# Down weights in output halves, a written-out layer loop and a router on column groups in a two-layer encoder

## The chip, the cores and the metric

The kernel runs on one core of one Trainium2 chip. The metric is the device time of one execution in microseconds. The kernel before took 2113.52 us, the median of three runs (2112.22 to 2116.02).

## The reference

The model has two layers on 256 tokens of 1024 numbers, all in float32. Each layer adds an attention branch and a long-convolution branch to x, and then an expert network. The part that the change touches is the second:

```python
def expert_choice_ffn(h, router_w, wg, wu, wd):       # h = rms_norm(x), 256 x 1024
    C = 32                                            # tokens per expert, 16 experts
    aff = softmax(h @ router_w)                       # 256 x 16
    gate, idx = top_k(aff of each expert over the tokens, C)
    xs = h[idx]                                       # 16 x 32 x 1024
    a = einsum('becd,edf->becf', xs, wg)              # f = 1408
    u = einsum('becd,edf->becf', xs, wu)
    o = einsum('becf,efd->becd', silu(a) * u, wd) * gate
    return zeros(256, 1024).at[idx].add(o)            # added to the tokens
```

Each expert chooses its 32 tokens; the three weight matrices of an expert (gate, up and down) hold 1024 x 1408 numbers each.

## The kernel before

The kernel is written engine by engine: each engine has a program of its own, with waits on semaphores between them. In each of these programs the layer loop is a hardware loop (`Fori(0, DEPTH)`), so a wait in it compares with a value worked out in registers, such as `L * 16 + 4 * it + 1`.

A layer has a dense part (latents, projections, attention, convolution by DFT, branches, output product) and an expert part. x stays in SBUF as two blocks of 128 tokens. The dense weights pass through a ring; the same memory holds an expert's gate and up weights later (`ring`), and `region` holds its down weights.

**Router** (lines 629 to 670). The normalized tokens are transposed block by block: DVE (L1200) and ACT (L892) write `aT`, eight blocks of 128 features by 256 tokens. L654 forms the logits as a product of 16 output rows, eight blocks accumulated in one bank, two records of TensorE for each block. DVE copies the 16 x 256 result (L1206), two transposes bring it back to tokens by experts (L660), softmax and top-k follow on DVE and ACT, and L670 and L1241 give the table from which L681 gathers the tokens of a group of four experts.

**Experts.** A loop over four groups holds four experts each, in TensorE's and DVE's programs; ACT and SP loop over the experts. For an expert TensorE forms gate and up products (L695) in 4 column groups of 32 (the 1408 columns are 3+3+3+2 blocks of 128), ACT takes silu (L920), DVE multiplies (L1262), three transposes (L709) and a DVE copy (L1266) give `hT`. The down product (L719) walks b = 0, 1, 2 over the 11 row blocks, 4 + 4 + 3, and for each b over both output halves c, 44 records in all (two for each of 22 products). For each b it waits for one piece of the down weights:

```python
for b in range(FB):
    pe.wait_ge(wd_in[b], 16 * n + 16)
    for c in range(2):
        for j in range(len(TILES[b])):
```

Then ACT copies output half 0 (L926) and DVE half 1 (L1268), and L734 combines: four products (eight records) with `gselT`, the gate values placed by token, in the order token block 0 halves 0 and 1, token block 1 halves 0 and 1. DVE adds each to x (L1273). The next layer's ACT program waits until the first two of the last four adds are done, issues three small loads for the filters (L762, L764), and squares the two token blocks (L769); the root (L772) releases DVE's reciprocal (L980).

**Loads.** SP issues the expert weights in this order: first half of gate of expert e when half of the gate product of e-1 is done, second half when all of it is, up (L272) when the up product is done, and the three down pieces (L278) when the down product is done (`o_psum`). The first down load of a layer goes out in the dense part, gate and up of expert 0 when the ring is free.

Of the kernel before, what the change touches and what calls it, by code (L numbers as in the profile page):

```python
# [14 lines left out]
ALU = mybir.AluOpType  # L15
# [4 lines left out]
P = 128  # L20
D, S, DEPTH = 1024, 256, 2
SB, DB = S // P, D // P
# [11 lines left out]
FB = 3  # L34
# [6 lines left out]
HW = 512  # L41
EPS = 1e-6
# [33 lines left out]
C_N = C_EPS + 1  # L76
# [14 lines left out]
W_N = DB + DB * E  # L91


def build(nc, x_in, vecs, fvecs, qkw_in, consts_in, decay_in, w_lat, w_q_b, units_in,
          filt12, filt3, w_gate, w_up, w_down, out):
    with ExitStack() as ctx:
# [70 lines left out]
        lgT = uT_t[0:E, 4096:4096 + S]  # L167
# [42 lines left out]
        wd = R[:, 0:NF_TILES * D].rearrange("p (r d) -> p r d", r=NF_TILES)  # L210
# [13 lines left out]
        o_psum o_act o_dve y2_psum x_dve""".split()  # L224
# [8 lines left out]
        def _(sp):  # L233
            sp.dma_start(x3, x_in.rearrange("a (b p) d -> p (a b) d", p=P)).then_inc(s["x_in"], 16)
            sp.dma_start(cst[:, :], consts_in).then_inc(s["consts_in"], 16)
            with sp.Fori(0, DEPTH) as L:
# [37 lines left out]
                def load_down(e):  # L274

                    for b in range(FB):
                        cols = slice(CT * D * b, CT * D * b + len(TILES[b]) * D)
                        sp.dma_start(R[:, cols], w_down[L * E + e, :, cols]).then_inc(wd_in[b], 16)  # L278
# [32 lines left out]
        def _(pool):  # L311
            with pool.Fori(0, DEPTH) as L:
# [32 lines left out]
        def _(pe):  # L345
# [5 lines left out]
            with pe.Fori(0, DEPTH) as L:  # L351
# [298 lines left out]
                for i in range(DB):  # L650
                    if i % 4 == 0:
                        pe.wait_ge(s["xn2T_dve"], 2 * L + 1 + i // 4)
                        pe.wait_ge(s["xn2T_act"], 2 * L + 1 + i // 4)
                    m = mm(bank(4, S, rows=E), fvec[:, W_RT + i * E:W_RT + (i + 1) * E], aT[:, i],  # L654
                           start=i == 0, stop=i == DB - 1)
# [3 lines left out]
                for t in range(SB):  # L659
                    m = tp(bank(5, E, t * E), lgT[:, t * P:(t + 1) * P], ident[0:E, 0:E])  # L660
# [13 lines left out]
                with pe.Fori(0, NG) as g:  # L674
# [11 lines left out]
                    for q in range(GROUP):  # L686
# [24 lines left out]

                        pe.wait_ge(s["hT_dve"], n + 1)
                        pe.wait_ge(s["o_act"], n + FREE)
                        pe.wait_ge(s["o_dve"], n + FREE)
                        for b in range(FB):
                            pe.wait_ge(wd_in[b], 16 * n + 16)
                            for c in range(2):
                                for j in range(len(TILES[b])):
                                    m = mm(bank(c, rows=CAP, row0=CAP * j),  # L719
                                           hT[:, b * P + CAP * j:b * P + CAP * (j + 1)],  # L720
                                           wd[:, CT * b + j, c * 512:(c + 1) * 512], start=b == 0,
                                           stop=j >= len(TILES[b + 1]) if b < FB - 1 else True)
                        m.then_inc(s["o_psum"], 1)

                        pe.wait_ge(s["gselT_act"], n + 1)
                        for k in range(4):
                            t, c = k // 2, k % 2
                            if k == 0:
                                pe.wait_ge(s["o_act"], n + 1 + FREE)
                            if k == 1:  # L730
                                pe.wait_ge(s["o_dve"], n + 1 + FREE)

                            pe.wait_ge(s["x_dve"], n * 4 + max(k - 1, 0) + X_FREE)
                            mm(bank(6 + k % 2), gselT[:, t * P:(t + 1) * P], o_sb[:, c * 512:(c + 1) * 512],  # L734
                               start=True, stop=True).then_inc(s["y2_psum"], 1)
# [3 lines left out]
        def _(act):  # L739
# [17 lines left out]
            with act.Fori(0, DEPTH) as L:  # L757
# [3 lines left out]
                act.wait_ge(s["x_dve"], L * E * 4 + X_FREE - 2)  # L761
# [154 lines left out]
                with act.Fori(0, E) as e:  # L916
                    n = L * E + e
                    act.wait_ge(s["gate_done"], n + 1 + FREE)
                    act.wait_ge(s["hid_dve"], n + FREE)
                    af(sil[:, 0:2 * P], bank(2, 2 * P), ACT.Silu)  # L920
                    af(sil[0:ROWS_LAST, 2 * P:FT], bank(2, P, 2 * P, rows=ROWS_LAST),
                       ACT.Silu).then_inc(s["sil_act"], 1)
                    act.wait_ge(s["gselT_psum"], n + 1)
                    af(gselT, bank(4, S), ACT.Copy).then_inc(s["gselT_act"], 1)  # L924
                    act.wait_ge(s["o_psum"], n + 1 + FREE)
                    af(o_sb[:, 0:512], bank(0), ACT.Copy).then_inc(s["o_act"], 1)  # L926
# [3 lines left out]
        def _(dve):  # L930
# [46 lines left out]
            with dve.Fori(0, DEPTH) as L:  # L977
# [228 lines left out]
                copy(lgT, bank(4, S, rows=E)).then_inc(s["lgT_dve"], 1)  # L1206
# [31 lines left out]
                with dve.Fori(0, NG) as g:  # L1238
# [13 lines left out]
                    for q in range(GROUP):  # L1252
# [14 lines left out]
                        dve.wait_ge(s["o_psum"], n + 1 + FREE)  # L1267
                        copy(o_sb[:, 512:1024], bank(1)).then_inc(s["o_dve"], 1)  # L1268
                        for k in range(4):
                            t, c = k // 2, k % 2  # L1270
                            dve.wait_ge(s["y2_psum"], n * 4 + k + 1)
                            xc = x3[:, t, c * 512:(c + 1) * 512]
                            tt(xc, xc, bank(6 + k % 2), ALU.add).then_inc(s["x_dve"], 1)  # L1273


def constants():
# [26 lines left out]
    c[:, C_EPS] = EPS  # L1303
    tau = np.abs(pos - S // 2) / f32(S // 2)
# [72 lines left out]
```

## Time and profile before

| | before |
|---|---|
| median of three runs | 2113.52 us |
| profiled execution | 2112.32 us |
| its span, first to last instruction | 2110.5 us |
| TensorE busy | 1606.2 us (76%) |
| DVE busy | 508.7 us (24%) |
| ACT busy | 287.6 us (14%) |
| moved by DMA | 644.83 MB, mean 306 GB/s |
| instructions recorded | 23405 |

The first layer runs to about 1055 us: its dense part ends at about 411 us, the router and the gather at about 433 us, and the experts fill the rest. The second layer repeats this. PE is TensorE's matmul record and PEld its weight load, which lies beside it; PEclk is the clock that TensorE was granted, 1.00 being full speed and 0.50 half. "Idle before" names what ended an engine's wait; where it says "issue", the engine waited for nothing that the profile shows.

### The profile page before, as it was taken

To read this page: it belongs to the slowest core of one execution; us is meant where nothing else is said; L and a number is where in the kernel's file an instruction comes from. 1 tells how busy PE (TensorE), PEld (TensorE's weight loads), DVE (VectorE), ACT (ScalarE), POOL (GpSimd) and SP (SyncE) were. 2 spreads that over 40 slices of the span, in tenths; PEclk is the share of its full clock that TensorE was granted. 3 is DMA by queue.
4 is the path that set the end of the run, shared out by engine and by line. 5 is a ranking of instruction groups with operands and counts; after the bars stand their busy time and mean duration, and the time that the engine had idled before them with its cause. 6 is when DMAs were issued, how large, how long until landed. Compare 5 with 4: busy or idle time off the path is not lost.

```text
span 2110.5 us, 23405 instructions
## 1 busy us (share of the span) xinstructions
PE 1606.2 (76%) x9552; PEld 909.9 (43%) x9552; DVE 508.7 (24%) x1057; ACT 287.6 (14%) x594; POOL 45.7 (2%) x24
## 2 busy tenths in 40 slices
PE   7999999876466566666689999997865665665665
PEld 4687688432232132232256866884322222321322
DVE  2654541111111111111126545402111111111111
ACT  2233200200000000000022332002000000000000
POOL 0300000000000000000002000000000000000000
PEclk9999999988788888878899999999887887888888
DMA  7522024679999999999945220246899999999997
GB/s 282 195 85 100 1 80 190 245 319 430 435 423 430 430 427 430 432 429 426 426 149 199 80 100 1 80 189 258 341 434 426 426 430 434 423 430 430 427 430 319
DMA packets 36352, 644.83 MB, mean 306 GB/s; under 512 B 3984, under 2 KB 4880, under 8 KB 6160
## 3 DMA queue, kind: packets, MB, share of 16 engines
q1 hardware_dynamic: 35472, 638.84, 72.2%
q10 hardware_dynamic: 768, 4.29, 0.7%
q8 instruction: 96, 1.57, 0.3%
q14 instruction: 16, 0.13, 0.0%
HBM read 642.07 MB, written 1.05 MB: 305 GB/s over the span
## 4 chain that ended last, share of the span: by engine, by line
PE 49%; DMA 42%; issue 4%; DVE 3%; DVEq 1%; SPq 1%; ACT 1%; ACTq 0%
DMA region<-w_down_dram 27%; DMA ring<-w_up_dram 15%; PE ps L695 7%; PE ps L394 7%; PE ps L619 5%; PE ps L461 5%; PE ps L719 3%; PE ps L644 3%; PE ps L552 2%; PE ps L681 2%; PE ps L587 2%; PE ps L577 2%; PE ps L422 2%; PE ps L484 1%; PE ps L439 1%
## 5 line engine op out<-in xcount | busy, mean ns | idle before, releaser
L695 PE MATMUL ps<-ring,uT 128*32 128x384 f32 (+1 forms) x4096 | 437.7, 567 | 296.8 <-DMA ring<-w_gate_dram 147.6
L695 PEld LDWEIGHTS ps<-ring,uT 128*32 128x32 f32 x4096 | 182.9, 130 | 550.6 <-issue 205.6
L719 PE MATMUL ps<-region,uT 128*32 128x512 f32 x1408 | 175.8, 596 | 34.9 <-DVE uT L1266 22.2
L1262 DVE TENSOR_TENSOR uT<-uT,ps 128x256 f32<-128x256 f32 x32 | 13.5, 421 | 699.4 <-PE ps L695 699.4
L394 PE MATMUL ps<-xnT,ring 128*128 128x256 f32 x768 | 178.3, 380 | 4.5 <-DVE uT L942 2.9
L394 PEld LDWEIGHTS ps<-xnT,ring 128*128 128x128 f32 x768 | 140.6, 190 | 24.1 <-DVE uT L942 4.5
L734 PE MATMUL ps<-uT 128*128 128x512 f32 x256 | 124.3, 618 | 28.8 <-ACT uT L926 28.8
L920 ACT ACT_TABLE_LOAD x32 | 41.1, 1283 | 631.3 <-PE ps L695 631.3
L461 PE MATMUL ps<-xnT,ring 128*128 128x256 f32 x512 | 115.0, 380 | 0.0
L719 PEld LDWEIGHTS ps<-region,uT 128*32 128x32 f32 x1408 | 44.5, 109 | 143.9 <-issue 105.3
L1273 DVE TENSOR_TENSOR x<-x,ps 128x512 f32<-128x512 f32 x128 | 87.9, 687 | 64.4 <-PE ps L734 64.4
L681 PE MATMUL ps<-uT,xnT 128*128 128x128 f32 x256 | 50.5, 381 | 68.2 <-issue 65.6
L461 PEld LDWEIGHTS ps<-xnT,ring 128*128 128x128 f32 x512 | 96.5, 190 | 13.7 <-issue 0.8
L734 PEld LDWEIGHTS ps<-uT 128*128 128x128 f32 x256 | 40.7, 188 | 114.9 <-issue 73.0
L681 PEld LDWEIGHTS ps<-uT,xnT 128*128 128x128 f32 x256 | 48.7, 294 | 73.7 <-issue 73.7
L1268 DVE COPY uT<-ps 128x512 f32<-128x512 f32 x32 | 22.1, 691 | 194.5 <-PE ps L719 194.5
L619 PE MATMUL ps<-uT,ring 128*128 128x256 f32 x256 | 57.9, 379 | 0.0
L619 PE MATMUL ps<-attnT,ring 128*128 128x256 f32 x256 | 57.9, 379 | 0.0
L644 PE MATMUL ps<-ring,uT 128*128 128x512 f32 x128 | 55.6, 592 | 0.0
L924 ACT ACTIVATE uT<-ps 128x256 f32<-128x256 f32 x32 | 12.3, 384 | 311.6 <-PE ps L703 311.6
L619 PEld LDWEIGHTS ps<-uT,ring 128*128 128x128 f32 x256 | 48.6, 190 | 6.6
L619 PEld LDWEIGHTS ps<-attnT,ring 128*128 128x128 f32 x256 | 48.6, 190 | 6.6
(195 smaller groups left out, 1368.1 us busy)
## 6 DMA issues: line engine op xcount, KB each, us to landing
ring<-w_gate_dram SPq DMA_DIRECT2D x64, 2816.0 KB, 28.4
ring<-w_up_dram SPq DMA_DIRECT2D x32, 5632.0 KB, 32.8
region<-w_down_dram SPq DMA_DIRECT2D x64, 2048.0 KB, 30.6
ring<-units_dram SPq DMA_DIRECT2D x34, 2048.0 KB, 8.0
region<-w_down_dram SPq DMA_DIRECT2D x32, 1536.0 KB, 37.2
ring<-w_lat_dram SPq DMA_DIRECT2D x4, 1344.0 KB, 20.6
ring<-w_q_b_dram SPq DMA_DIRECT2D x2, 2304.0 KB, 29.1
region<-filt_dram ACTq DMA_DIRECT2D x4, 512.0 KB, 11.9
```

Of the source, the lines that this page charges most:

```text
L394: m = mm(bank(b % 2, S), unit8(n)[:, i, j * P:(j + 1) * P], xnT[:, i], start=i == 0, stop=i == DB - 1)
L422: m = mm(bank((3 + g) % 7), latT[:, i, t * P:(t + 1) * P], m2[:, i, c * 512:(c + 1) * 512], start=i == 0, stop=i == QB - 1)
L461: m = mm(dst, unit8(7 + 4 * (i // 4) + g)[:, k, i % 4 * P:(i % 4 + 1) * P], xnT[:, k], start=k == 0, stop=k == DB - 1)
L552: m = mm(bank(5 + f), cst[:, C_F + t * NF + f * P:C_F + t * NF + (f + 1) * P], hflt[:, t], start=t == 0, stop=t == SB - 1)
L577: m = mm(bank(2 + f), cst[:, C_F + t * NF + f * P:C_F + t * NF + (f + 1) * P], z_t[:, c, t], start=t == 0, stop=t == SB - 1)
L619: m = mm(dst, unit8(n)[:, k, j * P:(j + 1) * P], (aT if g == 2 else uT)[:, k], start=k == 0, stop=k == DB - 1)
L644: m = mm(bank(4 + 2 * c + t), mT[:, k, t * P:(t + 1) * P], unit8(n)[:, k], start=k == 0, stop=k == DB - 1)
L681: m = mm(bank(i // 4, P, (i % 4) * P), xn2[:, t, i * P:(i + 1) * P], pick[:, t], start=t == 0, stop=t == SB - 1)
L695: m = mm(bank(b, QW[j], rows=CAP, row0=CAP * j), xs[:, i, q * CAP:(q + 1) * CAP], w[:, i, j * FT:j * FT + QW[j]], start=i == 0, stop=i == ...
L719: m = mm(bank(c, rows=CAP, row0=CAP * j), hT[:, b * P + CAP * j:b * P + CAP * (j + 1)], wd[:, CT * b + j, c * 512:(c + 1) * 512], start=b ...
L734: mm(bank(6 + k % 2), gselT[:, t * P:(t + 1) * P], o_sb[:, c * 512:(c + 1) * 512], start=True, stop=True).then_inc(s["y2_psum"], 1)
L1273: tt(xc, xc, bank(6 + k % 2), ALU.add).then_inc(s["x_dve"], 1)
```

## The change

It has three parts, and some that follow from them.

1. The down weights lie in memory by output halves (half, row block, column), and come in three pieces: all 11 row blocks of half 0; the first 8 of half 1; the last 3 of half 1. TensorE forms all of half 0, ACT copies it, TensorE combines it with both token blocks, and then comes half 1 in the same way with DVE's copy. The combination's order is now half 0 for token blocks 0 and 1, then half 1. ACT's first wait of a layer is for three of the last four adds.
2. `for L in range(DEPTH)` takes the place of the hardware loop in all five programs: the code of both layers stands one behind the other, and L is a constant. The loops over experts and groups stay.
3. The router's weights are padded from 16 to 32 columns. Feature block i goes to column group i % 4, so four partial sums stand in four groups of 32 rows; a product with a 128 x 16 matrix of zeros and ones adds them up and turns them at once, in place of the two transposes.

With this, the router weights and the constants get wider, and the reserved scratch memory for DMA descriptors goes down to 2048.

```diff
+WD_AT = [0, NF_TILES * HW, (NF_TILES + 2 * CT) * HW, 2 * NF_TILES * HW]
+C_SUM = C_EPS + 1
+C_N = C_SUM + E
+EP = 32
+W_N = DB + DB * EP
-        wd = R[:, 0:NF_TILES * D].rearrange("p (r d) -> p r d", r=NF_TILES)
+        wd = R[:, 0:NF_TILES * D].rearrange("p (c r d) -> p c r d", c=2, r=NF_TILES)
...
-            with sp.Fori(0, DEPTH) as L:
+            for L in range(DEPTH):
...
-                    for b in range(FB):
-                        cols = slice(CT * D * b, CT * D * b + len(TILES[b]) * D)
-                        sp.dma_start(R[:, cols], w_down[L * E + e, :, cols]).then_inc(wd_in[b], 16)
+                    for k in range(3):
+                        cols = slice(WD_AT[k], WD_AT[k + 1])
+                        sp.dma_start(R[:, cols], w_down[L * E + e, :, cols]).then_inc(wd_in[k], 16)
...
-                    m = mm(bank(4, S, rows=E), fvec[:, W_RT + i * E:W_RT + (i + 1) * E], aT[:, i],
-                           start=i == 0, stop=i == DB - 1)
+                    m = mm(bank(4, S, rows=EP, row0=EP * (i % 4)), fvec[:, W_RT + i * EP:W_RT + (i + 1) * EP], aT[:, i],
+                           start=i < 4, stop=i >= 4)
...
-                    m = tp(bank(5, E, t * E), lgT[:, t * P:(t + 1) * P], ident[0:E, 0:E])
+                    m = mm(bank(5, E, t * E), lgT[:, t * P:(t + 1) * P], cst[:, C_SUM:C_SUM + E], start=True, stop=True)
...
+                        def down(c, b):
+                            for j in range(len(TILES[b])):
+                                m = mm(bank(c, rows=CAP, row0=CAP * j),
+                                       hT[:, b * P + CAP * j:b * P + CAP * (j + 1)],
+                                       wd[:, c, CT * b + j], start=b == 0,
+                                       stop=j >= len(TILES[b + 1]) if b < FB - 1 else True)
+                            return m
+                        def combine(c):
+                            for t in range(SB):
+                                k = 2 * c + t
+                                pe.wait_ge(s["x_dve"], n * 4 + max(k - 1, 0) + X_FREE)
+                                mm(bank(6 + t), gselT[:, t * P:(t + 1) * P], o_sb[:, c * 512:(c + 1) * 512],
+                                   start=True, stop=True).then_inc(s["y2_psum"], 1)
                         pe.wait_ge(s["hT_dve"], n + 1)
                         pe.wait_ge(s["o_act"], n + FREE)
+                        pe.wait_ge(wd_in[0], 16 * n + 16)
+                        for b in range(FB):
+                            m = down(0, b)
+                        m.then_inc(s["oa_psum"], 1)
+                        pe.wait_ge(s["gselT_act"], n + 1)
+                        pe.wait_ge(s["o_act"], n + 1 + FREE)
+                        combine(0)
                         pe.wait_ge(s["o_dve"], n + FREE)
+                        pe.wait_ge(wd_in[1], 16 * n + 16)
                         for b in range(FB):
-                            pe.wait_ge(wd_in[b], 16 * n + 16)
...
+                            if b == FB - 1:
+                                pe.wait_ge(wd_in[2], 16 * n + 16)
+                            m = down(1, b)
                         m.then_inc(s["o_psum"], 1)
...
+                        pe.wait_ge(s["o_dve"], n + 1 + FREE)
+                        combine(1)
...
-                act.wait_ge(s["x_dve"], L * E * 4 + X_FREE - 2)
+                act.wait_ge(s["x_dve"], L * E * 4 + X_FREE - 1)
...
-                    act.wait_ge(s["o_psum"], n + 1 + FREE)
+                    act.wait_ge(s["oa_psum"], n + 1)
...
-                copy(lgT, bank(4, S, rows=E)).then_inc(s["lgT_dve"], 1)
+                copy(lgT, bank(4, S)).then_inc(s["lgT_dve"], 1)
...
-    nc = bacc.Bacc("TRN2", target_bir_lowering=False, num_devices=1)
+    nc = bacc.Bacc("TRN2", target_bir_lowering=False, num_devices=1, dynamic_dma_scratch_size=2048)
```

## Rows read from the trace of the kernel before

**Rows 1.** The page's DMA load, mean busy share in 40 equal slices of the span.
```profile
DMA  7522024679999999999945220246899999999997
```
**Rows 2.** By stage: window, length, busy us (records) of five engines, PEclk, DMA, GB/s.
```profile
91.00:192.00 101.00, 100.22 (x545) 83.19 (x545) 53.43 (x127) 39.51 (x107) 0.00 (x0) 1.00 0.24 86
...
432.90:1047.80 614.90, 396.60 (x3038) 158.99 (x3038) 83.16 (x166) 44.34 (x79) 0.00 (x0) 0.84 1.00 426
1047.80:1062.46 14.66, 5.79 (x20) 1.66 (x21) 5.02 (x8) 4.57 (x8) 0.00 (x0) 0.87 1.02 376
```
**Rows 3.** The chain of waits, two loads of down weights: start, us, what.
```profile
604.81 37.34 DMA region<-w_down_dram
...
645.19 37.53 DMA region<-w_down_dram
```
**Rows 4.** Windows of 4 us ahead of the first expert, columns as in rows 2.
```profile
424.00:428.00 4.00, 2.50 (x12) 2.45 (x13) 0.73 (x4) 0.00 (x0) 0.00 (x0) 0.50 0.02 4
428.00:432.00 4.00, 3.89 (x24) 3.70 (x23) 0.76 (x2) 0.00 (x0) 0.00 (x0) 0.68 0.00 0
```
**Rows 5.** Timeline, router to first expert: start, us, engine, line, what, [idle before].
```profile
410.78 3.61 PE L654 MATMUL ps<-attnT,fvec 128*16 128x256 f32 x16 [0.17 <-issue]
411.33 0.84 ACT L892 ACTIVATE attnT<-ps,fvec 128x256 f32<-128x256 f32 x2
...
414.43 0.41 DVE L1206 COPY uT<-ps 16x256 f32<-16x256 f32 x1 [1.70 <-PE ps L654]
...
414.99 0.27 PE L660 MATMUL ps<-consts,uT 16*128 16x16 f32 x2 [0.60 <-DVE uT L1206]
...
425.87 6.03 PE L681 MATMUL ps<-uT,xnT 128*128 128x128 f32 x32 [1.31 <-DVE uT L1241]
...
432.86 10.52 PE L695 MATMUL ps<-ring,uT 128*32 128x384 f32 x128 [0.97 <-DVE uT L1248]
```
**Rows 6.** Groups by line and shape: busy us, mean ns of one, idle before.
```profile
L695 PE MATMUL ps<-ring,uT 128*32 128x256 f32 x1024 | 373.1, 487 | 0.0
...
L719 PE MATMUL ps<-region,uT 128*32 128x512 f32 x1408 | 175.8, 596 | 34.9 <-DVE uT L1266 22.2 <-DMA region<-w_down_dram 12.4
```
**Rows 7.** Timeline, last expert of layer one and start of layer two.
```profile
1043.53 3.64 PE L719 MATMUL ps<-region,uT 128*32 128x512 f32 x32 [0.69 <-DVE uT L1266]
...
1047.79 1.92 PE L719 MATMUL ps<-region,uT 128*32 128x512 f32 x12 [0.63 <-DMA region<-w_down_dram]
...
1049.77 0.60 ACT L926 ACTIVATE uT<-ps 128x512 f32<-128x512 f32 x1 [7.49 <-PE ps L719]
...
1050.60 3.88 PE L734 MATMUL ps<-uT 128*128 128x512 f32 x8 [0.90 <-ACT uT L926]
...
1051.76 0.69 DVE L1273 TENSOR_TENSOR x<-x,ps 128x512 f32<-128x512 f32 x1 [1.30 <-PE ps L734]
...
1052.62 0.69 DVE L1273 TENSOR_TENSOR x<-x,ps 128x512 f32<-128x512 f32 x1 [0.17 <-PE ps L734]
...
1053.48 0.51 ACTq L762 DMA_DIRECT2D region<-filt_dram  x1
...
1054.53 0.69 DVE L1273 TENSOR_TENSOR x<-x,ps 128x512 f32<-128x512 f32 x1 [0.17 <-PE ps L734]
1055.33 1.06 ACT L769 ACTIVATE work<-x 128x1024 f32<-128x1024 f32 x1 [3.45 <-DVE x L1273]
...
1057.59 0.30 ACT L772 ACTIVATE small<-small,consts 128x2 f32<-128x2 f32 x1
1060.73 0.17 DVE L980 RECIPROCAL small<-small 128x2 f32<-128x2 f32 x1 [5.52 <-issue]
```
**Rows 8.** Timeline, the last expert of layer two.
```profile
2094.65 3.64 PE L719 MATMUL ps<-region,uT 128*32 128x512 f32 x32 [0.69 <-DVE uT L1266]
...
2098.58 1.92 PE L719 MATMUL ps<-region,uT 128*32 128x512 f32 x12 [0.29 <-DMA region<-w_down_dram]
...
2105.41 0.69 DVE L1273 TENSOR_TENSOR x<-x,ps 128x512 f32<-128x512 f32 x1 [0.17 <-PE ps L734]
```

More of the change, by code:

```diff
@@ L166, in build @@
         hT = uT_t[:, 2816 + 2 * FT:2816 + 3 * FT]
-        lgT = uT_t[0:E, 4096:4096 + S]
+        lgT = uT_t[:, 4096:4096 + S]
         work = uT_t[0:E, 4352:4352 + S]
@@ L223, in build @@
         pick_dve xs_psum xs_dve gsel_dve gselT_psum gselT_act gate_half gate_done up_done sil_act hid_dve hT_psum hT_dve
[L224 removed]
+        oa_psum o_psum o_act o_dve y2_psum x_dve""".split()
         s = {n: sem(n) for n in names}
@@ L311, in _ @@
         def _(pool):
-            with pool.Fori(0, DEPTH) as L:
+            for L in range(DEPTH):
                 pool.wait_ge(s["qkw_scaled"], L + 1)
@@ L350, in _ @@
                 pe.sem_inc(s[n], FREE)
-            with pe.Fori(0, DEPTH) as L:
+            for L in range(DEPTH):
                 pe.wait_ge(s["consts_in"], 16)
@@ L717, in _ @@
[L717 to L722, printed above, removed]
-                        m.then_inc(s["o_psum"], 1)
@@ L725, in _ @@
[L725 to L735, printed above, removed]
+                            if b == FB - 1:
+                                pe.wait_ge(wd_in[2], 16 * n + 16)
@@ L756, in _ @@
                 act.sem_inc(s[n], FREE)
-            with act.Fori(0, DEPTH) as L:
+            for L in range(DEPTH):
                 load_sqrt_table()
-                act.wait_ge(s["x_dve"], L * E * 4 + X_FREE - 2)
+                act.wait_ge(s["x_dve"], L * E * 4 + X_FREE - 1)
                 act.dma_start(w12, filt12[L]).then_inc(s["filt_in"], 16)
@@ L976, in _ @@
             dve.sem_inc(s["x_dve"], X_FREE)
-            with dve.Fori(0, DEPTH) as L:
+            for L in range(DEPTH):
                 dve.wait_ge(s["norm1_rms"], L + 1)
@@ L1266, in _ @@
                         copy(hT[:, 0:2 * P + ROWS_LAST], bank(5, 2 * P + ROWS_LAST)).then_inc(s["hT_dve"], 1)
[L1267 to L1273, printed above, removed]
+                        for c in range(2):
+                            if c == 1:
+                                dve.wait_ge(s["o_psum"], n + 1 + FREE)
+                                copy(o_sb[:, 512:1024], bank(1)).then_inc(s["o_dve"], 1)
+                            for t in range(SB):
+                                dve.wait_ge(s["y2_psum"], n * 4 + 2 * c + t + 1)
+                                xc = x3[:, t, c * 512:(c + 1) * 512]
+                                tt(xc, xc, bank(6 + t), ALU.add).then_inc(s["x_dve"], 1)
 def constants():
@@ L1303, in constants @@
     c[:, C_EPS] = EPS
+    c[:, C_SUM:C_SUM + E] = np.arange(P)[:, None] % EP == np.arange(E)[None]
     tau = np.abs(pos - S // 2) / f32(S // 2)
@@ L1330, in k_major_experts, with by_halves @@
         return w.transpose(0, 2, 1, 3).reshape(DEPTH * E, P, -1)
+    def by_halves(w):
+        return w.reshape(DEPTH * E, P, NF_TILES, 2, HW).transpose(0, 1, 3, 2, 4).reshape(DEPTH * E, P, -1)
     small = np.zeros((DEPTH, P, 4), np.float32)
@@ L1337 @@
                            cols(a["filt_skip"].reshape(DEPTH, -1)), small], 2)
-    fvecs = np.concatenate([cols(a["norm2_w"]), k_major(a["router_w"]).reshape(DEPTH, P, -1)], 2)
+    router = np.pad(k_major(a["router_w"]), ((0, 0), (0, 0), (0, 0), (0, EP - E)))
+    fvecs = np.concatenate([cols(a["norm2_w"]), router.reshape(DEPTH, P, -1)], 2)
     qkw = np.concatenate([a["q_norm_w"], a["k_norm_w"]], 1)
@@ L1364 @@
         "w_gate": k_major_experts(a["expert_w_gate"], range(DB)), "w_up": k_major_experts(a["expert_w_up"], range(DB)),
-        "w_down": k_major_experts(a["expert_w_down"], [r for tiles in TILES for r in tiles]),
+        "w_down": by_halves(k_major_experts(a["expert_w_down"], [r for tiles in TILES for r in tiles])),
     }
-    nc = bacc.Bacc("TRN2", target_bir_lowering=False, num_devices=1)
+    nc = bacc.Bacc("TRN2", target_bir_lowering=False, num_devices=1, dynamic_dma_scratch_size=2048)
     arrays, args = {}, []
```

2 lines of the change are left out of this document (removed).

## The prediction

> **What bounds the kernel now.** I read the load row of the page first: the DMA queues are full from about 440 to 1050 us and again from about 1490 to the end [rows 1]. The table by stage then splits a layer in two. In the dense part TensorE is the bound: 100.2 of 101.0 us in the attention stretch. In the expert part the DMA is: 614.9 us at a DMA share of 1.00 and 426 GB/s, TensorE busy 396.6 of them [rows 2]. The chain of waits agrees: it runs from one load of down weights to the next, issued at 604.81 and at 645.19, 40.38 us apart [rows 3]. Each spends 37.3 us from issue to landing, nearly all behind the gate and up weights of its queue: an expert moves 3 x 5.77 MB = 17.3 MB, and 17.3 MB at 426 GB/s are 40.6 us. So inside the 15 refills of a layer only bytes count, and the change keeps the bytes and the number of pieces.
>
> Time can therefore move in three places: where TensorE, DVE and ACT hand the router's result on while the DMA idles (0.02 and 0.00 share in the two windows [rows 4]), behind the last landing of each layer, and at the border between the layers.
>
> **The router.** The stream of expert weights starts when half of the first gate product is done, so the router's microseconds count one for one. Before, 16 records take 3.61 us from 410.78, so they end at 414.39 [rows 5]. In four column groups the first eight have their inputs at once. The last eight wait for the scaled copies of ACT, two blocks from 411.33 to 412.17 [rows 5]. What eight records of 128x256 in column groups cost is not shown alone. Bounds: one record's 0.49 us if all overlap [rows 6], and 8 x 3.61/16 = 1.81 us if nothing does. Between them stands the first expert, 128 such records in 10.52 us, 0.082 each [rows 5]: seven more behind the first give 0.49 + 0.57 = 1.06, which I take. The end is then 412.2 + 1.06 = 413.3, 1.1 us sooner (bounds 1.7 and 0.4). The two small transposes become two products with full-height weights, four records for two: 0.27 us [rows 5] becomes 0.54, so +0.3 (between 0 and, at 0.23 a record, +0.6). DVE's copy grows in partitions, not in length: nothing. Net -0.85 us a layer, -1.7 in all, from -3.4 to about +0.4. If the four groups bring nothing, the second half also starts at 412.6, not 412.2.
>
> The Trainium skill (TensorEngine Tiling (Array Packing), Theoretical Speedup) gives up to 4x for a dimension of 32 or less. By it 3.61 us would become 0.9 and 2.7 us a layer would go; the ACT copy that ends at 412.17 is why I don't follow it: the engine could be four times faster and still not have its input.
>
> The granted clock blurs this. It is 0.50 in 424 to 428 and 0.68 in 428 to 432 [rows 4]: the upper level came back in mid-gather, about 4.6 us into the 6.03 us that start at 425.87. If it comes back at the same moment after a gather that starts earlier, the gather's head start is spent at half rate, and a layer keeps 0.4 of 0.85 us; if it comes back from the start, up to 2.3 us more go. On average I leave the 0.85.
>
> **Down weights by output halves.** Per expert the bytes are the same (5.77 MB), in pieces of 2.88, 2.10 and 0.79 MB for 2.10, 2.10 and 1.57. So at 426 GB/s the first half lands 6.8 us ahead of the end, the second piece 1.9 us ahead. In 15 of 16 experts all this lies beside a full DMA. In the last of each layer it is on the path, so I schedule TensorE there [rows 7].
> - Today: 32 records from 1043.53, which end at 1047.17; the last piece is in at 1047.79, 12 records take 1.92; ACT copies 0.60; the combination starts at 1050.60, and its four adds end at 1055.22.
> - After: the first half, 22 records. A record takes (3.64 - 0.59)/31 = 0.098 us, the last 0.59 [rows 6, 7]; so 2.66 us, 1043.53 to 1046.19. Handoff 0.06 and ACT copy 0.60: 1046.85. Handoff 0.23: the first combination starts at 1047.08. Four of the eight records: 1.94, to 1049.02. Only then come the second half's 22 records, queued behind the combination: 2.66, to 1051.68. Its weights landed at 1047.79, so they have waited for TensorE, not it for them. Handoff 0.06, DVE copy 0.69 (as an add of that shape), handoff 0.23: 1052.66. First add 1.16 later, 1053.82 to 1054.51; the second 0.86 after it, ending at 1055.37.
>
> That is 0.15 us later than today's 1055.22. The halves save the combination's first 1.94 us behind the landing, but they bring a wait for ACT's copy (0.89 us) into the middle of TensorE's order. hT is ready only 4.26 us before the last landing, and the first half with its combination needs 5.5. In the last layer it is ready 3.93 us before [rows 8]: 2094.65 + 11.84 = 2106.49 against 2106.10, +0.4 us. Queued behind the added wait is the second half, and behind that SP, which issues the next expert's down load about 1.9 us later than now; gate and up weights (11.5 MB, 27 us at 426 GB/s) cover this.
>
> **The border of the layers.** Today DVE ends its last add at 1055.22 and then waits for no semaphore that the profile shows: its reciprocal starts at 1060.73, "issue" [rows 7], though ACT's square root was done at about 1057.9: the first square at 1055.33, two of 1.06 with their accumulator reads (0.19 each, overlapped by 0.1), the root of 0.30. I read this as fetching the loop's first instructions after the jump back. Written out, DVE has no jump there. Then the roots decide. ACT's filter loads wait for the first token block: today that is the second add, ended 1053.31, issue at 1053.48, squares at 1055.33, 2.0 us behind the add. After, the first block is complete with the third add, 1054.51, so squares start at 1056.53, the root ends at 1059.1, DVE starts at about 1059.2: -1.5 us. If the stall stays, it starts with the later add and costs +0.15. TensorE's own jump lies under the wait for DVE and gives nothing.
>
> The Trainium skill (Runtime: NRT & Kernel Launch, Instruction fetch mechanics) says that a taken branch out of the two resident pages stalls on a fetch and that straight code is prefetched. By it the 5.5 us of DVE vanish whole, and TensorE's too; the sum keeps 1.5 of them, since ACT is late next.
>
> **Constants for register sums in waits.** The sums are formed while the engine still waits, and TensorE fills 99% of the attention stretch: nothing, at best 1 us in all. Wider router weights and constants add 64 KB and 8 KB of loads: under 0.1 us. The smaller scratch buffer serves no queue that the page lists.
>
> **Sum**, against the profiled execution (span 2110.5, 1.8 around it, 2112.32): -1.7 + 0.4 - 1.5 = -2.8 us (the first layer's end is inside the border's -1.5). That execution is 1.2 below the median of 2113.52, which I shift: 2110.7.
>
> **Rivals.**
> - The halves work as drawn: the first is combined before the second lands. Then only 3 x 2 records (about 1.0 against 1.92 us) and half the combination (1.94) follow the landing: 0.9 + 1.9 a layer, 5.6 in all, so near 2105. For it: the first half does land 6.8 us early. Against: hT starts at 1043.53, too late for 5.5 us of work. With a clock that returns early in the gather the same time is reached otherwise.
> - The stall moves rather than goes: DVE falls out of its expert loop into code not yet fetched. Then -1.7 + 0.4 + 0.15, near 2112.4.
> - Slower by late loads: SP issues down(e+1) only when the second half is done, 1.9 us later in each of 15 refills per layer. If the 37.3 us from issue to landing were latency, not queueing, the period of 40.38 us would grow by 1.9: 30 x 1.9 = +57 us, near 2170. It decides once the delay eats the queue behind it, 27 us of gate and up weights. Against: DMA share 1.00.
> - Slower by code: twice the pages, and a second copy of loops at another place in them. A loop that straddles what is resident stalls by DVE's 5.5 us per pass; in the expert part that is hidden for a few, in a dense part each such stall shows. One or two: +5 to +11, near 2118.
>
> **How the numbers follow.** My case has 0.50, the moved stall 0.14, the working halves or an early clock 0.24, late loads 0.04, code stalls 0.08. About 0.2%, 4.2 us, is what this measurement tells from no change, so faster means below 2109.3: the working halves or early clock, and the quarter of my case in which the clock favours one gather by 1.5 us or more: 0.36. Slower (above 2117.7): 0.04 and most of the code case, 0.09. Same: 0.55. The range for 8 in 10 goes from 2105.0 (halves work) to 2115.5 (router bounds at their bad end, moved stall, a bad clock in one gather).
>
> **What would show it.** Right: the same 40.3 to 40.4 us between down loads; the router's product ending about 1 us behind ACT's last scaled copy, set by that copy; in the last expert of a layer TensorE's second half starting after the first combination and after its weights landed; DVE without "issue" at the border. Wrong: a DMA share under 0.98 in the expert part, a gap between the first combination and the second half that waits for the DMA, new idle on "issue" in the second layer's dense part, or a dense part shorter by more than 1 us.

## The result and the profile after

The changed kernel takes 2101.66 us (median of 11 runs, 2098.29 to 2109.72), the kernel before 2112.26 (11 runs, 2109.29 to 2116.02). The ratio is 0.995, 95% interval 0.9937 to 0.9963: 10.6 us faster, between 7.8 and 13.3. The forecast was 2110.7 us, 2.8 us faster than the median then known, in a range from 2105.0 to 2115.5. The direction was right; the size was not. The time lies outside the range, and below 2109.3, where the prediction saw a chance of 0.36. The profiled execution took 2101.75 us, 10.6 less than the one of before.

Both profiled executions are divided at the same events: TensorE's first router product, its first gather product, its first gate product, the last packet of the layer's last up load, and the next layer's first transpose.

| stretch, us | before | after | change | forecast |
|---|---|---|---|---|
| start to router, layer one | 410.78 | 413.23 | +2.45 | 0 |
| router to gather | 15.09 | 14.16 | -0.93 | -0.85 |
| gather to first gate product | 6.99 | 7.60 | +0.61 | clock |
| first gate product to last up packet | 600.90 | 599.00 | -1.91 | 0 |
| to the first transpose of layer two | 28.69 | 26.68 | -2.01 | -1.5 |
| to router, layer two | 399.33 | 396.50 | -2.83 | 0 |
| router to gather | 15.07 | 13.93 | -1.14 | -0.85 |
| gather to first gate product | 7.15 | 6.34 | -0.81 | clock |
| first gate product to last up packet | 600.67 | 596.00 | -4.67 | 0 |
| to the end | 25.86 | 26.51 | +0.65 | +0.4 |

Together, what I had priced (router, border and end) came close to its price: -3.4 us for -2.8. What I had priced at nothing, the stretch in which the DMA is full, gave 6.6 us. The dense parts moved by +2.5 and -2.8 and cancel; over the 14 profiled kernels of this study they lie between 409.7 and 414.9 us and between 396.2 and 402.4, whatever the kernel.

The page's section on the DMA queues has what I had passed over. The instruction queue, packets, MB and share of 16 engines, before:

```profile
q8 instruction: 96, 1.57, 0.3%
```

and after:

```profile
q8 instruction: 48, 0.79, 0.2%
```

The packets are 16 KB each, and each takes 1.07 us (the median in the kernel before). Before, 30 of them lie in the 14 periods between the up weights of the layer's second expert and those of its last, in both layers; after, 12 in layer one and 4 in layer two. The length of these 14 periods can be read from the waits of TensorE's up product, which starts when the last part of the up load is in. The timeline of the kernel before (start, us, engine, line, what, idle before and what ended it), layer one and layer two:

```profile
466.18 3.42 PE L695 MATMUL ps<-ring,uT 128*32 128x384 f32 x22 [5.30 <-DMA ring<-w_up_dram]
...
1034.25 7.24 PE L695 MATMUL ps<-ring,uT 128*32 128x384 f32 x62 [6.24 <-DMA ring<-w_up_dram]
...
1517.47 2.14 PE L695 MATMUL ps<-ring,uT 128*32 128x384 f32 x13 [5.45 <-DMA ring<-w_up_dram]
...
2085.20 2.36 PE L695 MATMUL ps<-ring,uT 128*32 128x384 f32 x14 [6.08 <-DMA ring<-w_up_dram]
```

568.07 and 567.73 us. The same of the changed kernel, where the line is L698:

```profile
468.56 0.86 PE L698 MATMUL ps<-ring,uT 128*32 128x384 f32 x4 [4.53 <-DMA ring<-w_up_dram]
...
1034.47 6.82 PE L698 MATMUL ps<-ring,uT 128*32 128x384 f32 x64 [6.67 <-DMA ring<-w_up_dram]
...
1510.86 7.05 PE L698 MATMUL ps<-ring,uT 128*32 128x384 f32 x64 [4.36 <-DMA ring<-w_up_dram]
...
2073.94 7.61 PE L698 MATMUL ps<-ring,uT 128*32 128x384 f32 x64 [5.88 <-DMA ring<-w_up_dram]
```

565.91 and 563.08 us. The DMA is full in both ([rows 2] for before; the windows of after, columns as there):

```profile
434.99:1043.30 608.31, 390.16 (x3004) 152.17 (x3004) 83.10 (x167) 44.32 (x79) 0.00 (x0) 0.86 1.00 426
1477.44:2083.60 606.16, 392.85 (x3006) 151.91 (x3006) 83.11 (x167) 44.32 (x79) 0.00 (x0) 0.86 1.00 427
```

Where is the difference, if the DMA is full in both? In the spread over its 16 engines. The first packet of the up loads comes every 40.2 us in both kernels (before: 450.74 for expert 1, 1013.43 for expert 15, 562.7 us over 14). The last packet falls behind: before it comes 14.9 us after the first for expert 1 (465.68) and 20.3 us after it for expert 15 (1033.77). A load is complete only when its slowest part is in: expert 15's lands at 1034.20, and TensorE's product starts at 1034.25. A mean share of 1.00 does not show how far that part is behind.

The trace has 16 landing events for each up load, and they show the spread directly. Before, those of expert 1 in layer one lie within 1.7 us. Those of expert 15 lie in two groups: eight within 1.4 us, and eight that come 6.1 to 6.9 us after the first; layer two shows the same (1.4, and 6.2 to 6.8). In the changed kernel, layer one has eight within 0.4 us, one at 1.7, six at 3.2 to 3.5 and one at 5.0 us; in layer two all 16 lie within 1.9 us. So half of the parts fall behind, and further in the kernel with more packets.

TensorE's own fetch stalls went with the packets. The gather's group of the page, before:

```profile
L681 PE MATMUL ps<-uT,xnT 128*128 128x128 f32 x256 | 50.5, 381 | 68.2 <-issue 65.6
```

and after:

```profile
L684 PE MATMUL ps<-uT,xnT 128*128 128x128 f32 x256 | 37.0, 312 | 15.9 <-DVE uT L1253 9.3
```

The last expert of layer one and the border, in the timeline of after. These lines answer to [rows 7]:

```profile
1043.32 2.78 PE L717 MATMUL ps<-region,uT 128*32 128x512 f32 x22 [0.69 <-DVE uT L1278]
...
1046.99 1.98 PE L727 MATMUL ps<-uT 128*128 128x512 f32 x4 [0.89 <-ACT uT L938]
...
1048.90 2.77 PE L717 MATMUL ps<-region,uT 128*32 128x512 f32 x22
...
1051.73 0.69 DVE L1282 COPY uT<-ps 128x512 f32<-128x512 f32 x1 [2.04 <-PE ps L717]
...
1058.85 0.17 DVE L992 RECIPROCAL small<-small 128x2 f32<-128x2 f32 x1 [3.59 <-ACT small L784]
```

The second half's products start right behind the first combination, with no wait for weights, as scheduled. DVE's wait is now for ACT's root and no longer for "issue".

The router's product in layer one of the changed kernel, its second eight records and the four that add the partial sums up:

```profile
414.77 0.64 PE L657 MATMUL ps<-attnT,fvec 128*32 128x256 f32 x8 [0.89 <-ACT attnT L904]
...
416.03 0.81 PE L663 MATMUL ps<-consts,uT 128*128 128x16 f32 x4 [0.63 <-DVE uT L1218]
```

### The profile page after: what moved, and what is told of

It reads as the page before. It is cut to its first block, busy times and chain, and to the rows that moved or that the text cites. A ratio compares the mean times of both kernels' runs of the same rounds, so it can differ in the third digit from the quotient of the medians.

```text
span 2100.0 us, 22784 instructions
## 1 busy us (share of the span) xinstructions
PE 1600.1 (76%) x9556; PEld 896.8 (43%) x9556; DVE 508.3 (24%) x1057; ACT 287.4 (14%) x594; POOL 45.7 (2%) x24
## 4 chain that ended last, share of the span: by engine, by line
PE 48%; DMA 47%; DVE 2%; ACT 1%; DVEq 1%; issue 1%; SPq 0%; ACTq 0%
DMA ring<-w_up_dram 46%; PE ps L698 12%; PE ps L397 7%; PE ps L622 5%; PE ps L464 5%; PE ps L647 3%; PE ps L555 2%; PE ps L590 2%; PE ps L580 2%; PE ps L425 2%; PE ps L487 1%; PE ps L442 1%; PE ps L370 1%; DMA ring<-w_lat_dram 1%; PE ps L511 1%; PE ps L479 1%
## 5 line engine op out<-in xcount | busy, mean ns | idle before, releaser
L698 PE MATMUL ps<-ring,uT 128*32 128x384 f32 (+1 forms) x4096 | 446.5, 575 | 330.2 <-DMA ring<-w_up_dram 182.2
L698 PEld LDWEIGHTS ps<-ring,uT 128*32 128x32 f32 x4096 | 182.7, 132 | 593.0 <-issue 212.0
L464 PEld LDWEIGHTS ps<-xnT,ring 128*128 128x128 f32 x512 | 96.5, 190 | 13.7 <-issue 0.8
L684 PE MATMUL ps<-uT,xnT 128*128 128x128 f32 x256 | 37.0, 312 | 15.9 <-DVE uT L1253 9.3
L555 PE MATMUL ps<-work,consts 128*128 128x512 f32 x96 | 45.0, 620 | 4.1 <-DVE work L1120 4.1
L590 PE MATMUL ps<-consts,work 128*128 128x256 f32 x192 | 43.0, 380 | 2.3 <-DVE work L1166 2.3
```

What stands on the lines that cost most here:

```text
L464: m = mm(dst, unit8(7 + 4 * (i // 4) + g)[:, k, i % 4 * P:(i % 4 + 1) * P], xnT[:, k], start=k == 0, stop=k == DB - 1)
L555: m = mm(bank(5 + f), cst[:, C_F + t * NF + f * P:C_F + t * NF + (f + 1) * P], hflt[:, t], start=t == 0, stop=t == SB - 1)
L590: m = mm(bank(5 + j // 2, S, (j % 2) * S), yT_t[:, f, j * P:(j + 1) * P], cst[:, C_IF + f * S:C_IF + (f + 1) * S], start=f == 0, stop=f == 2)
L698: m = mm(bank(b, QW[j], rows=CAP, row0=CAP * j), xs[:, i, q * CAP:(q + 1) * CAP], w[:, i, j * FT:j * FT + QW[j]], start=i == 0, stop=i == ...
```

## The experiments

**The theory after the result.** TensorE's loop over the four groups has some 1600 instructions. Before, it is fetched again in each pass, nine packets a group (30 in the 14 periods). These packets go through the DMA engines that carry the weights, unevenly, and the weight loads wait for the engine that fell behind. Written out, the layer loop puts the group loop elsewhere, and its instructions mostly stay. **Rivals:** the new sizes and order of the down pieces level the engines; the register sums and jumps of the other engines; the gather's stalls themselves.

**One part alone: the layer loop.**

```diff
-            with pe.Fori(0, DEPTH) as L:
+            for L in range(DEPTH):
```

(the same on all five engines)

> The kernel before with the layer loop alone written out, on all five engines; down weights and router as before. Theory (instruction fetches of TensorE's group loop take turns on the DMA engines that carry the weights, and written out the loop lies otherwise and keeps its instructions): most of the gain is here, -7 to -9 us against before, instruction packets near 48 for 96, and the 14 periods between the last packets of up weights take 563 to 566 us for 568. Rival (the new sizes and order of the down pieces even out the DMA engines): only the border gains, -1 to -3 us, 96 instruction packets, 568 us.

2098.69 us (2095.28 to 2107.49, 6 runs) against 2112.29: ratio 0.9939 (0.9924 to 0.9954), -13.6 us. The profile has 57 instruction packets; 21 lie in layer one's 14 periods and 4 in layer two's, which take 568.9 and 563.2 us. The gain is larger than the 7 to 9 expected, and as far as the intervals tell, the loop is the whole of it. But 568.9 us lies outside the 563 to 566 expected: 21 packets take longer here than 30 before. The landing events of expert 15's up load say why. Eight lie within 0.4 us, six at 4.7 to 5.1, one at 6.1 and the last at 8.0 us, where before none is later than 6.9. It is the slowest part that counts, not the number of packets. The six runs fall in two groups, 2095 to 2099 and 2105 to 2107; the profiled one, with fetches in two of layer one's groups, is of the slower.

**One part alone: the halves.** The down weights and the order of products and adds as changed; loops and router as before.

> The kernel before with the down weights by output halves alone; layer loops in hardware, router as before. Theory (fetches): no gain, between -0.5 and +1 us, 96 instruction packets, 568 us for the 14 periods. Rival (piece sizes even out the engines): -5 to -7 us, with 563 to 566 us for the 14 periods and still 96 instruction packets.

2111.69 us (11 runs), ratio 0.9999 (0.999 to 1.0007): nothing, as the schedule of the last expert had it. The rival falls: 568.1 us with 30 packets in layer one. In layer two there are 566.2 us with 21, and 87 packets in all instead of the 96 expected: the last group kept its instructions there, though both layers run the same loop.

**The same code, half a page further on.**

```diff
             for n in ("gate_done", "up_done", "o_psum"):
                 pe.sem_inc(s[n], FREE)
+            for _ in range(256):
+                pe.wait_ge(s["one_dve"], 1)
```

Two of these waits share an instruction, so 128 are added, in front of the layer loop.

> The kernel before with 128 idle instructions put in front of TensorE's layer loop, where it waits 13 us for the first tokens anyway: all its code lies half a fetched page (16 KB, 256 instructions) further on, nothing else changes. Theory (where the group loop lies on the pages decides whether it stays): the count of instruction packets changes from 96 and the time with it, by up to -7 us at 50 packets; if 128 is the wrong shift, both stay. Rival (piece sizes, or the constants in the waits): nothing changes, within 1 us, 96 packets or 97.

2102.43 us (2101.56 to 2104.17, 5 runs), ratio 0.9955 (0.9942 to 0.9968): -9.9 us, where up to -7 was expected. This is the kernel before with nothing but idle waits added, and it has nearly the whole gain. 42 instruction packets, 4 in the 14 periods of each layer, 563.1 and 563.3 us. Its up products in layer two:

```profile
1512.88 6.43 PE L697 MATMUL ps<-ring,uT 128*32 128x384 f32 x46 [5.42 <-DMA ring<-w_up_dram]
...
2076.21 7.98 PE L697 MATMUL ps<-ring,uT 128*32 128x384 f32 x64 [5.51 <-DMA ring<-w_up_dram]
```

Register sums, down pieces and router are the same as before here, so none of them is needed for the gain.

**A loop that fits anywhere.** TensorE loops over the expert too, about 400 instructions; DVE first copies the expert's 32 tokens to a fixed place, from which the products read.

```diff
-                    for q in range(GROUP):
+                    with pe.Fori(0, GROUP) as q:
...
+                        dve.wait_ge(s["up_done"], n + FREE)
+                        copy(xe, xs[:, :, q * CAP:(q + 1) * CAP]).then_inc(s["xe_dve"], 1)
```

> The changed kernel with TensorE's four experts of a group as a loop of about 400 instructions in place of 1600 written out; DVE copies the 32 tokens of the expert to a fixed place first (one copy of 128x256, 0.3 to 0.5 us, beside the DMA). Theory (fetches): no instruction packet in the expert part, both layers' 14 periods at 40.2 us each, 563 us; -10.6 us of the change goes to about -12.5 against before. Rival: the copy adds to each expert and the fetches did not matter: as the changed kernel or up to 1 us slower than it.

2103.33 us (2098.53 to 2104.81, 5 runs), ratio 0.9959 (0.9946 to 0.9972). No packet in the 14 periods, 562.9 and 563.1 us, as expected. The total is not below the changed kernel's: -9.0 us against before, where I had said -12.5. The intervals of the two overlap widely. What zero packets save over 12 and 4 is 3 us in the periods of one layer. The forecast of the total missed; that of the periods held.

**Wholly written out.**

```diff
-                with pe.Fori(0, NG) as g:
+                for g in range(NG):
```

> The changed kernel with TensorE's loop over the four groups written out too: 20622 instructions in one line, no jump, each of them fetched once. Theory (fetches beside full weight queues cost the time): 23 to 26 instruction packets inside the 14 periods of each layer come back, the periods take 565 to 568 us each instead of 563, and the kernel gives back 3 to 8 us of the 10.6. Rival (the jumps cost the time: TensorE's stalls ahead of each gather): without a jump it is 0 to 3 us faster than the changed kernel.

2102.87 us (6 runs), ratio 0.9954 (0.9941 to 0.9966). 76 packets, 21 in each layer's 14 periods, 566.0 and 566.2 us: the fetches and the 3 us a layer are back, in both layers, without a jump. Its up products in layer two:

```profile
1508.84 8.30 PE L698 MATMUL ps<-ring,uT 128*32 128x384 f32 x64 [4.82 <-DMA ring<-w_up_dram]
...
2075.07 6.80 PE L698 MATMUL ps<-ring,uT 128*32 128x384 f32 x64 [6.69 <-DMA ring<-w_up_dram]
```

But in total it gives back 1 us or nothing against the changed kernel, not 3 to 8, since that one has 565.9 us in layer one itself. The rival (without jumps it is faster) is not borne out either. TensorE's stalls are gone in this run: ahead of the gather it has no idle time on "issue" (139.2 us in 26 waits before, weight loads and products together). The periods are long all the same, so the stalls at the gather are not what lengthens them.

The Trainium skill (Runtime: NRT & Kernel Launch, Instruction fetch mechanics) calls the cost of crossing a 16 KB boundary mostly hidden and takes full unrolling as the preferred form. Hidden for TensorE it is here; for the weights beside it, these periods are 3 us longer than those of the small loop. By the same section of the Trainium skill only two blocks of 256 instructions are held, and a taken branch out of them fetches. By that rule a loop of some 1600 is fetched in every pass. The nine packets in each pass of the kernel before agree. The shifted kernel doesn't: in both layers the last three passes of its group loop have no packet at all. Here the measurement decides: such a loop can stay. The same section of the Trainium skill gives TensorE's instruction memory room for 2048 instructions. That would hold this loop, but it doesn't say why the loop is fetched in one kernel and not in the other.

**TensorE alone, and all but TensorE.** The layer loop written out on one engine, and on the other four.

> The kernel before with the layer loop written out on TensorE alone; DVE, ACT, SP and GpSimd keep theirs. Theory: the fetches of TensorE's group loop are what counts, -7 to -11 us, and DVE's stall of 5.5 us at the border stays. Rival (DVE's or SP's jumps and register sums matter): less than half of the -13.6 of the run with all five loops written out.

2103.79 us (2099.95 to 2109.01, 6 runs), ratio 0.9953 (0.9937 to 0.9968): -10.1 us, 39 packets, 563.2 us in both layers. DVE's 5.4 us of "issue" at the border are still there.

> The kernel before with the layer loop written out on DVE, ACT, SP and GpSimd, and left on TensorE. Theory: only DVE's wait at the border goes, the part behind it 1.5 to 3 us shorter, 96 instruction packets and 568 us as before; -1.5 to -3.5 us in all. Rival (register sums and code of the other engines count): -8 us or more.

2110.77 us (11 runs), ratio 0.9984 (0.9976 to 0.9993): -2.8 us, 96 packets, 568.0 and 567.7 us. From the last up packet to the next layer it takes 26.56 us for 28.69. At the border DVE's reciprocal starts at 1059.49 after a wait of 2.54 us for ACT's root, no longer on "issue".

So the -13.6 split into about -10 for TensorE's layer loop, whose fetches go, and -3 for the layer loops of the other four engines; the border became 2.1 us shorter with these. -10.1 and -2.8 add up to -12.9.

**The price of a packet.** The kernel with the small loop fetches nothing in the 14 periods. ACT adds two loads of one row of 12 KB per expert, and waits for each before its next; they are no part of the computation.

```diff
+                    act.dma_start(W[0:1, 0:3072], w_gate[n, 0:1, 0:3072]).then_inc(s["pk"], 16)
```

> The kernel with the small expert loop, which fetches nothing in the expert part, with two loads of one row of 12 KB per expert from ACT's queue to memory that nobody reads then: 28 in the 14 periods, as the kernel before had 30 fetches. The loads are not part of the computation. Theory (a packet on one engine holds up the weights behind it, and each load waits for its slowest engine): the periods grow from 563 to 566 to 569 us per layer, more if the same engine gets them all (28 x 0.46 us = 13 us more), and the kernel is 6 to 13 us slower than with the small loop alone. Rival (only the sum of bytes counts: 28 x 12 KB = 0.3 MB): under 1 us per layer.

2124.74 us (2123.43 to 2127.98, 5 runs), 21.4 us above the small loop's 2103.33 (20.2 if each is taken against the kernel before of its own round). Expected were 6 to 13 us. The ratio to before is 1.0059 (1.0046 to 1.0072). The periods take 575.1 and 574.9 us. Up products in layer one, without the loads:

```profile
463.65 5.58 PE L699 MATMUL ps<-ring,uT 128*32 128x384 f32 x47 [3.05 <-DMA ring<-w_up_dram]
...
1026.67 7.36 PE L699 MATMUL ps<-ring,uT 128*32 128x384 f32 x64 [6.12 <-DMA ring<-w_up_dram]
```

and with them:

```profile
466.76 2.46 PE L699 MATMUL ps<-ring,uT 128*32 128x384 f32 x30 [2.96 <-DMA ring<-w_up_dram]
...
1041.87 7.30 PE L699 MATMUL ps<-ring,uT 128*32 128x384 f32 x64 [6.19 <-DMA ring<-w_up_dram]
```

563.0 and 575.1 us: 12.1 more for 28 packets of 0.46 us, whose sum is 12.9. That is the case in which one engine gets them all, 13 us a layer by what was expected; spread over 16, the 0.34 MB would be 0.8 us by the 426 GB/s of the stretch, an estimate. The landing events of expert 15's up load show the one engine: 15 of the 16 lie within 1.5 us (2.2 in layer two), and the last comes 13.7 us after the first (14.0). The up loads' first packets still come every 40.2 us. The Trainium skill (DMA: Bandwidth & Descriptors, Why a DMA increments its semaphore by 16 and not by 1) says that a load issued by SP or ACT which runs on only some of the 16 engines goes to the lowest-numbered ones. Loads that take one engine each would then all meet on the same one, and the single late part agrees.

For TensorE's fetches, 30 packets of 1.07 us, 32 us in sum, cost 5.0 us (568.1 for 563.1), above the 2.0 of an even spread and far below one engine's 32. Shared among the eight that fall behind, they would be 4.0 us each, an estimate; 21 packets would be 2.8, and the run written out straight shows about 3.

**The changed kernel, shifted.** The same 128 idle instructions.

> The changed kernel with 128 idle instructions in front of TensorE's code, as in the shifted kernel before. Theory: position decides; the changed kernel still fetched 12 packets in the 14 periods of layer one (one group out of three) and 4 in layer two. Shifted, the count changes: down to 4 and 4, and 1 to 3 us faster, or back up to 30 in either layer and 2 to 5 us slower for it. Rival: nothing within 1 us, 48 packets.

2105.72 us (2103.96 to 2110.11, 6 runs), ratio 0.9965 (0.9951 to 0.9978). Position decided again: 40 packets for 48, 4 and 4 in the periods, 563.0 and 563.2 us. The total went the other way: 8.2 us below before, where 1 to 3 us better than the changed kernel's 10.6 was expected. In its profile the dense part of layer two is 402.4 us for 396.5: the load of the decay table, which stands on the path there, took 7.0 us from issue to landing for 4.9 (6.0 in the kernel before). Whether the shift causes this or chance, one profile doesn't say.

**The router alone.**

> The kernel before with the router on column groups alone. Theory: from the start of its product to the gather 14.2 us for 15.1 in each layer, -1.7 us in all, packets and periods as before. Rival (the changed position of the code by the two added records counts too): another count of packets than 96, and -3 us or more with it.

2110.64 us (11 runs), ratio 0.9989 (0.9979 to 0.9998), -2.9 us with an interval that holds the -1.7 expected. Router to gather 13.83 and 14.00 us for 15.1; 96 packets, 567.7 and 568.0 us.

**A better order.** My schedule says what is wrong with the halves: the first combination stands ahead of products whose weights have landed.

```diff
-                        combine(0)
...
                         m.then_inc(s["o_psum"], 1)
+                        combine(0)
                         pe.wait_ge(s["o_dve"], n + 1 + FREE)
                         combine(1)
```

(DVE copies before its four adds)

> The changed kernel with TensorE's order in an expert: first half, second half, and only then both combinations; DVE's adds after its copy. By the schedule of the last expert the second half starts about 2.7 us sooner, ends at the last landing plus about 1.1, and the last add comes 2.5 us sooner at each layer's end: -4 to -5 us against the changed kernel, if the border passes all of it on. Rival (the border and the end hang on something else): under 1 us.

2096.68 us (2095.66 to 2101.07, 6 runs) against 2113.92, ratio 0.9926 (0.9912 to 0.9939): -17.2 us, 5.0 below the changed kernel, and the best of the study. It takes 25.08 us from the last up packet to the next layer and 24.92 to the end (26.68 and 26.51 in the changed kernel). The 44 records now run through; timeline, last expert of layer one:

```profile
1039.89 5.35 PE L717 MATMUL ps<-region,uT 128*32 128x512 f32 x44 [0.69 <-DVE uT L1278]
```

That is 3.2 us of the 5.0, where I had said 4 to 5; the rest is within the spread of medians.

> The changed kernel with both: TensorE's expert loop of about 400 instructions, and both halves' products ahead of both combinations. No fetch in the expert part (both layers 563 us for the 14 periods) and 1.6 us less behind each last up load: about 2 us below the run with the second half first, -18 to -20 us against before. Rival (what is left of the fetches costs nothing, as they are few): the same as the run with the second half first, -17.

2098.01 us (2094.48 to 2100.97, 6 runs), ratio 0.9929 (0.9917 to 0.9941): the same as with the better order alone. No packets in the periods, 563.0 and 563.2 us, but no 2 us less in total. The rival held: once most fetches are gone, the rest can't be told from the spread.

## Why the prediction was wrong

- **"inside the 15 refills of a layer only bytes count"** is the step that failed: the prediction put this stretch at nothing, and it gave 6.6 of the 10.6 us. With it fell "TensorE's own jump lies under the wait for DVE and gives nothing": its layer loop alone, written out, gives -10.1 us. I took the mean share of 1.00 as proof that the stretch can't get shorter. It says that 16 engines are busy on average; the weights wait for the last of them. What else goes through these engines was on the page (96 instruction packets), and I had looked at jumps only for the stall of the engine that jumps. The kernel shifted by 128 idle instructions shows the step wrong: -9.9 us with nothing else changed.
- **The bytes seemed to fit exactly.** 17.3 MB at 426 GB/s are 40.6 us, and one pair of down loads was 40.38 apart. The first packets of the up loads come every 40.19 us in the same trace, and the last ones every 40.58 on average (568.07 over 14). The difference of 0.4 us a load is what the step missed. Of the signs of being wrong, the DMA share stayed at 1.00 and would not have shown it; a dense part shorter by more than 1 us did occur (-2.8 in layer two), but lies within the spread of all the profiles.
- **Rival "slower by code"** named the right mechanism, where a loop lies in the blocks of code that are fetched, with the wrong sign and place. The loops were fetched in every pass before, and written out they mostly stay. The prediction priced the stall of an engine, which it took as hidden in the expert part. The 65.6 us of "issue" at the gather are such stalls, and it was the packets fetched in them and after them that cost time.
- **Router**: -0.85 us forecast, -0.93 and -1.14 measured, in part by luck. As drawn, the second eight records wait for ACT's copy: ACT was the limit. They took 0.64 us where I took 1.06, so the product ends 2.2 us after its start for 3.6 before, 1.4 sooner and not 1.1. The four records that add the sums up took 0.81 us where I took 0.54. The two errors cancel.
- **Halves**: forecast +0.15 and +0.4 us at the two ends; alone they give -0.6 us of 2112 (interval -2.1 to +1.5), which tells neither from nothing. The second half started at 1048.90 (forecast 1049.02), its copy at 1051.73 (1051.74), from a start 0.2 us earlier.
- **Border**: -1.5 us forecast, -2.0 from the last up packet on. DVE started at 1058.85, forecast 1059.2. Written out on the four engines other than TensorE, the loop gave -2.8 in total (-1.5 to -5.1).
- **Late loads** didn't matter, as argued. Measured from the first packet of the same expert's up load, SP issues expert 1's down load 3.0 us later than before, and over all experts of a layer 1.1 and 0.1 us later on average, not 1.9. The period between the up loads' first packets stays 40.2 us.
- **Clock and dense parts**: the range allowed 2.3 us for a clock that favours one gather. The dense parts vary by more, which I had not counted: 5.2 us between profiles in layer one and 6.2 in layer two.

What stays open: why the same program keeps the group loop's instructions in one group or run and not in another (12 packets in layer one and 4 in layer two of the same profile; 30 and 21 with the halves alone), and by what rule the fetches go to half of the engines, as the landing events suggest. The runs show that position changes how many there are, not by what rule. The totals also don't follow the periods down to the last microseconds: the changed kernel when shifted and the two with the small loop have the shortest periods and not the lowest times for it. It is not shown either that the sum of the parts (-13.6, -0.6 and -2.9, together -17.1) should be -10.6; their intervals just allow it.

## What to carry to other kernels

Where a stretch is bound by DMA and its share is at 1.00, look at the spread over the engines. Compare the period of a load's first packet with that of its last, look at how far its landing events lie apart, and count every small packet beside the weights, instruction fetches above all. A big hardware loop on TensorE may be fetched anew in each pass; a smaller body, or only another position, takes the fetches away, and a kernel's time can move by half a per cent from a change that adds nothing. Where work is put in the middle of an engine's order to use a wait, schedule the last pass: if the wait isn't there then, the inserted work is ahead of something that is ready.

## What the hardware showed that I had not expected

- 128 idle instructions ahead of a loop made the kernel 9.9 us faster, by 4 instruction packets in the periods for 30.
- 28 loads of 12 KB, all in the one late part of the load, made 563.0 us of full traffic 575.1: nearly their whole time, with 0.1% of the bytes.
- The cost of fetches is not proportional to their number: 30 packets 568.1 us, 21 packets 566.0 and 566.2 written out straight but 568.9 with the layer loop written out alone, 12 packets 565.9, 4 packets 563.1 to 563.3, none 562.9 to 563.1. It follows the slowest of the 16 parts: 6.9 us behind the first in the 568.1, 8.0 in the 568.9, 5.2 in the 566.0.
- TensorE's loop of some 1600 instructions is fetched in every pass of one kernel (nine packets), and in none of the last three passes of the same kernel with 128 idle instructions ahead.
